# Moving 74 of the 266 weight-residual subtractions from VectorE to GpSimd in a two-layer encoder kernel

## The reference

```python
def trunk(x, p, ...):
    for i in range(DEPTH):                       # DEPTH = 2
        if i % N_MIXERS == 0:                    # layer 0: gated short convolution, two big matmuls
            y, nh = short_conv_mixer(x, conv_states[j], a_w_in[j], a_conv_w[j], a_w_out[j])
        else:                                    # layer 1: trailing means over 2/4/8/16 frames, small matmuls
            y, nh = pool_mixer(x, pool_states[j], pos0, b_w_grp[j], b_scale[j])
        h = layer_norm(ALPHA * x + y, ln1_g[i], ln1_b[i])
        r = jax.nn.relu(h @ mlp_w1[i])           # 1024 -> 4096
        f = (r * r) @ mlp_w2[i]                  # 4096 -> 1024
        e = (p[i] @ ple_w[i]) * jax.nn.sigmoid(h @ ple_gate_w[i])
        x = layer_norm(ALPHA * h + f + e, ln2_g[i], ln2_b[i])
```

## Time and profile before

| | |
|---|---|
| time, median of 3 runs | 2246.59 us (2242.61 to 2251.49) |
| the profiled execution | 2246.59 us, span 2244.8 us |
| PE busy | 2144.8 us (96%), 13166 matmuls |
| DVE busy | 1237.4 us (55%) |
| ACT busy | 779.6 us (35%) |
| POOL busy | 72.9 us (3%) |
| mean granted PE clock | 0.982 of 2.4 GHz |

### The profile page before, as it was taken

How to read it: one execution, slowest core, us unless ns; L and a number is a source line. 1 busy time by engine, 2 the same in 40 slices (tenths; PEclk the granted TensorE clock), 3 DMA queues, 4 the chain that set the end, 5 groups by cost and what they waited for, 6 DMA issues and landing times.

```text
span 2244.8 us, 32406 instructions
## 1 busy us (share of the span) xinstructions
PE 2144.8 (96%) x13166; PEld 2124.4 (95%) x13166; DVE 1237.4 (55%) x1795; ACT 779.6 (35%) x1203; POOL 72.9 (3%) x61
## 2 busy tenths in 40 slices
PE   8999999899999999999998988789999999999987
PEld 8999999899999999999998988789999999999986
DVE  4233368753444434445667879894354444444587
ACT  3222134542232222234443555353233332223354
POOL 0000000000000000000002003200000000000000
PEclk9999999999999999999999999899999999999998
DMA  4011142321111111113312233233122211112232
GB/s 164 29 56 53 41 132 69 104 92 57 57 57 38 50 43 48 46 47 118 127 48 63 83 119 93 66 102 100 57 76 66 66 57 57 38 57 75 76 112 97
DMA packets 47403, 164.69 MB, mean 73 GB/s; under 512 B 7488, under 2 KB 7616, under 8 KB 47296
## 3 DMA queue, kind: packets, MB, share of 16 engines
q1 hardware_dynamic: 45216, 163.04, 22.9%
q10 hardware_dynamic: 2080, 0.12, 0.1%
HBM read 158.68 MB, written 4.46 MB: 73 GB/s over the span
## 4 chain that ended last, share of the span: by engine, by line
PE 81%; DVE 13%; ACT 4%; issue 2%; DMA 0%; ACTq 0%; DVEq 0%
PE ps L645 27%; PE ps L647 27%; PE ps L646 27%; DVE w_split L571 3%; ACT w_split L750 1%; DVE acc L990 1%; DVE acc L1007 1%; DVE acc L1070 1%; DVE ln_squares L959 1%; DVE std L999 1%; ACT acc L809 1%; DVE win L1023 1%; DVE r_lo L1066 1%; DVE ln_squares L960 0%; DVE h_hi L1029 0%
## 5 line engine op out<-in xcount | busy, mean ns | idle before, releaser
L645 PE MATMUL ps<-h_hi,w_split 128*128 128x352 f32 x2160 | 701.8, 325 | 24.6 <-DVE w_split L571 10.5
L647 PE MATMUL ps<-h_hi,w_split 128*128 128x352 f32 x2160 | 695.2, 322 | 0.0
L646 PE MATMUL ps<-h_lo,w_split 128*128 128x352 f32 x2160 | 695.1, 322 | 0.0
L645 PE MATMUL ps<-r_hi,w_split 128*128 128x352 f32 x1632 | 541.4, 332 | 40.5 <-DVE acc L1070 38.2
L646 PE MATMUL ps<-r_lo,w_split 128*128 128x352 f32 x1632 | 530.5, 325 | 0.0
L647 PE MATMUL ps<-r_hi,w_split 128*128 128x352 f32 x1632 | 530.1, 325 | 0.0
L1070 DVE TENSOR_TENSOR acc<-acc,ps 128x352 f32<-128x352 f32 x768 | 375.2, 518 | 144.0 <-PE ps L647 143.2
L645 PEld LDWEIGHTS ps<-h_hi,w_split 128*128 128x128 f32 x2160 | 407.5, 189 | 28.2 <-issue 12.7
L646 PEld LDWEIGHTS ps<-h_lo,w_split 128*128 128x128 f32 x2160 | 408.5, 189 | 0.4
L647 PEld LDWEIGHTS ps<-h_hi,w_split 128*128 128x128 f32 x2160 | 407.8, 189 | 0.0
L571 DVE TENSOR_TENSOR w_split<-w_raw,w_split 128x1024 fp32r<-128x1024 f32 x266 | 323.9, 1236 | 118.3 <-ACT w_split L750 118.1
(11 more groups left out here) (80 smaller groups left out, 1131.8 us busy)
## 6 DMA issues: line engine op xcount, KB each, us to landing
w_raw<-w_stream SPq DMA_DIRECT2D x290, 512.0 KB, 3.7
x_raw<-x_t SPq DMA_DIRECT2D x6, 704.0 KB, 8.5
y_t<-acc SPq DMA_DIRECT2D x4, 704.0 KB, 4.5
w_raw<-p_t SPq DMA_DIRECT2D x6, 352.0 KB, 2.9
y_t<-acc SPq DMA_DIRECT2D x4, 352.0 KB, 2.2
pool_new<-acc ACTq DMA_DIRECT2D x2, 60.0 KB, 5.8
vec<-vectors SPq DMA_DIRECT2D x1, 78.0 KB, 7.2
pool_history<-pool_hist SPq DMA_DIRECT2D x1, 60.0 KB, 6.9
```

The source lines that it names most:

```text
L645: pe.matmul(out, wh, mov_h, start=first, stop=False)
L646: pe.matmul(out, wh, mov_l, start=False, stop=False)
L647: return pe.matmul(out, wl, mov_h, start=False, stop=last)
```

## The change

Two of the three tables that say which engine subtracts are changed. The call sites that use `dve` stay as they are.

```diff
-    dve, both, first_two = (lambda j: "dve"), (lambda j: "dve"), (lambda j: "dve")
+    dve, both, first_two = (lambda j: "dve"), (lambda j: ("dve", "pool")[j % 2]), (lambda j: ("pool", "dve")[j // 2])
```

## The result

The changed kernel took 2260.36 us (median of 11 runs, 2254.62 to 2278.09) and the kernel before 2248.05 (11 runs, 2242.61 to 2255.11): a ratio of 1.006, 95% interval 1.004 to 1.0081, or +13.5 us (+9 to +18). The forecast was 2246 us, from a sum of -0.8; the measured time lies at the upper end of the whole range told (2231 to 2262) and outside that of the likeliest case (2237 to 2256).

A forecast was written before the change was run, and what follows sets the result against it. DVE was taken to set the end in the norm and pooling stages, PE everywhere else. Terms -3.9 - 3.1 + 2.6 + 1.5 + 1.3 + 0.8 = -0.8 us took 2246.6 to 2245.8, told as 2246 us, range 2231 to 2262.

The forecast's parts named there:

- the likeliest case: Whole kernel: 2246 us, own range 2237 to 2256, chance 0.56.
- last norms: From 2130 to 2200 us: a unit ahead of a sum costs 0.9, one behind wins 1.2; 0 (-1.2 to +1).
- gates of layer 0: Gate stage paced by DVE: subtraction and its wait leave DVE's loop, PE restarts earlier; -3.9 us (-5.5 to -2).
- quiet stretches: 475 to 1100 and 1515 to 2120 us, where PE never waits: 36 moved subtractions change nothing, 0 us.
- first norm, with its clock: First norm between the layers: POOL's turns delay the sum PE waits for, +2.6 us, and a lower clock follows, +1.5.
- pooling of group 0: A subtraction ahead of the four window additions at 1186.59 lengthens the DVE chain beside them; +1.3 us (-1.2 to +2).
- gates of layer 1: Second gate stage: the same gain with other norms beside it, partly hidden behind ACT; -3.1 us (-5 to -1).
- long stretch, groups 1 and 2: 1344 to 1486 us, pooling and norms: 12 units leave DVE, -14.8, POOL's lock returns 15.6; +0.8 us (-14.8 to +5.6).
- the duration: POOL's time for one moved subtraction, scaled by elements from a window addition of 732 elements at 1.40 us: 1.96 us.
- The price of the lock: DVE time lost to each POOL subtraction: 0 to 1.7 us, taken as 1.3 in the stretch of groups 1 and 2.
- so its time is PE's time: 1344 to 1486 us: DVE is busy 130.6 of 142 us, so 12 subtractions leaving it count fully for PE, -14.8.
- The second rival: Between 1105 and 1515 us POOL starts early and holds up DVE's sums and products, 1.7 us each; 2263 us, chance 0.18.

The follow-up runs named there:

- e13: The changed kernel with ALU.add instead of ALU.subtract in POOL's 74 instructions; 2261.6 us, ratio to before 1.0029 to 1.0066.
- e14: The changed kernel with the raw buffer as both inputs of POOL's subtraction; 2242.07 us (one run).
- e15: The changed kernel with POOL's subtraction written over two rows of 512 elements; 2259.17 us (one run).
- e9: The changed kernel with each of the 74 POOL subtractions written as two instructions of 512 columns; 2256.66 us, ratio to before 0.9997 to 1.0036.
- e7: The changed kernel with each of the 74 POOL subtractions written as four instructions of 256 columns; 2244.33 us, ratio to before 0.9959 to 1.0002.
- e12: The kernel before with only the window additions each written as two instructions; 2246.13 us, ratio to before 0.996 to 0.9997.
- e10: The kernel before with 8 gate subtractions, in quarters, and 10 at the last norms, whole, moved to POOL; 2235.95 us, ratio to before 0.9923 to 0.997.
- e11: As e10, with each window addition also written as two instructions; 2231.34 us, ratio to before 0.9879 to 0.9936.
- e8: The changed kernel with POOL subtracting only 840 of 1024 columns, the rest of the residual left out; 2248.11 us, ratio to before 0.9988 to 1.0011.
- e1: The kernel before with only the 8 subtractions of the two gate stages moved to POOL; 2242.03 us, ratio to before 0.9939 to 0.9985.
- e4: The changed kernel with the 22 subtractions in the visits between the layers given back to DVE; 2244.91 us, ratio to before 0.9958 to 1.0004.
- e5: As e4, plus 22 extra POOL subtractions of the same size, each started once DVE has done that unit itself; 2264.3 us (one run).
- e3: The changed kernel, but each POOL subtraction also waits until DVE reaches its old place in the order; 2256.78 us, ratio to before 1.0016 to 1.0064.
- e6: As e5, but the 22 extra POOL instructions are memsets of the raw buffer, which write SBUF and read nothing; 2240.34 us (one run).

## Why the subtraction takes 2.39 us

**e13_add**, **e14_same** and **e15_two_rows** each make POOL's instruction like a window addition in one respect. In e13 and e14 the `lo` part of these weights is not the residual. Shown are the instruction's arguments alone, the last line in short:

```diff
-ws[:, slot, 1, :], raw[:, u.q, :], f32(ws[:, slot, 0, :]), ALU.subtract
+ws[:, slot, 1, :], raw[:, u.q, :], f32(ws[:, slot, 0, :]), ALU.add        # e13
+ws[:, slot, 1, :], raw[:, u.q, :], raw[:, u.q, :], ALU.subtract           # e14
+all three .rearrange("p (a t) -> p a t", a=2), ALU.subtract               # e15
```

> The changed kernel with ALU.add instead of ALU.subtract in GpSimd's 74 instructions (so the residual part of these weights is wrong). If the operation is what makes the subtraction dearer per element than the window additions (128x256, 512, 840, 1024 took 0.73, 1.27, 1.96, 2.38 us, 2.15 ns an element; window additions of 366 and 732 took 0.80 and 1.40, 1.64 ns an element), it takes 1.9 us and the kernel 2246 to 2250 us. If not, 2.39 us and 2257 to 2263 us.

> The changed kernel with the raw buffer as both inputs of GpSimd's subtraction (so the residual part of these weights is zero). If two inputs from tensors far apart cost more than two from one, it takes 1.9 us; if not, 2.39.

> The changed kernel with GpSimd's subtraction written over two rows of 512 elements, as the window additions go over two rows of 366. If the shape matters, 1.9 us; I expect 2.39, as the pieces of 256 and 512 had the same cost per element.

POOL's group from 500 to 1000 of e14, then of e15, e9 and e7:

```profile
L1162 POOL TENSOR_TENSOR w_split<-w_raw 128x1024 fp32r<-128x1024 f32 x2 | 3.8, 1896 | 156.9 <-ACT w_split L750 156.9
```

```profile
L1163 POOL TENSOR_TENSOR w_split<-w_raw,w_split 128x1024 fp32r<-128x1024 f32 x2 | 4.8, 2394 | 155.9 <-ACT w_split L750 155.9
```

```profile
L578 POOL TENSOR_TENSOR w_split<-w_raw,w_split 128x512 fp32r<-128x512 f32 x4 | 5.1, 1292 | 155.3 <-ACT w_split L757 155.3
```

```profile
L578 POOL TENSOR_TENSOR w_split<-w_raw,w_split 128x256 fp32r<-128x256 f32 x8 | 5.6, 738 | 154.8 <-ACT w_split L757 154.8
```

Neither the operation (e13: 2.39 us too) nor the shape matters; the inputs do. With one tensor as both inputs the instruction takes 1.90 us. The window additions read one tensor twice, shifted; a subtraction reads two tensors far apart. Subtractions grow by 2.15 ns an element ((2.39 - 0.74) / 768) above a base of 0.19 us, window additions by (1.40 - 0.80) / 366 = 1.64 (0.80 us for one of 366 elements in e12). Whether it is the distance of the two addresses or the tensor was not tried.

## A version that beats both

**e10_gates_last** keeps on POOL the 8 units of the gates, in quarters, and the 10 at the last norms, whole. **e11_windows_too** also writes each window addition as two instructions, and **e12_windows** does only that, in the kernel before.

```diff
-                    ins = pool.tensor_tensor(dst[:, :, have:end], src[:, :, have:end], src[:, :, have - lag:end - lag], ALU.add)
+                    for b in range(2):
+                        ins = pool.tensor_tensor(dst[:, b, have:end], src[:, b, have:end], src[:, b, have - lag:end - lag], ALU.add)
```

> Only the 8 subtractions of the gate stages (in quarters) and the 10 at the last norms (whole) are on GpSimd, the other 56 are back on VectorE. Sum from the earlier traces: gates in quarters -5.8 and -5.2 + 0.9, last norms -3.0, nothing between the layers: -13 us, some 2236 us. Rival: the quarters win in the gates only together with the units between the layers, then -6 - 3, 2239 us.

> As the kernel with gates and last norms on GpSimd, and each of the 30 window additions, which stood on GpSimd before as well, written as two instructions, one for each of its two blocks (366 elements instead of 732). Theory F: VectorE's waits behind them (18 instructions longer by 22.3 us between 1340 and 1500 before) come down by a third or more; PE gets back 3 to 8 us there, 2228 to 2233 us. Rival H (the window chain itself is late, and two instructions take longer than one): PE waits for the group matmuls, 0 to +5 us.

> The kernel before with nothing but the window additions in two pieces. Theory F: the same 3 to 8 us as beside the moved subtractions, 2240 to 2245 us. Rival H: 2248 or slower.

e10 came out as summed up, 2235.95 for 2236; by the ratio it wins 11.9 us (7 to 17) for the 13 expected. The windows in halves win 5.2 us between beside e10 and 6.4 by themselves (4.7, 1 to 9, by the ratio of e12), and DVE's waits behind them fall from 32.9 to 28.1 us although there are 49 of them for 27. e11 is the fastest kernel seen, 2231.34 us, 0.9% under the kernel before.

## Why the forecast was wrong, by its own steps

Each term by the starts of PE's matmuls, in us. e13 and e15 are two more executions with a POOL instruction of 2.39 us; e8 and e14 have one of 1.99 and 1.90, the forecast's duration (1.96) put to the test.

| term | forecast | changed (e13, e15) | e8, e14 | e7 |
|---|---|---|---|---|
| gates of layer 0 | -3.9 | -3.5 (-3.5, -3.5) | -4.5, -4.8 | -6.6 |
| quiet stretches | 0 | 0.0 (1.2, 0.0) | 5.1, 0.0 | 1.2 |
| first norm, with its clock | +2.6 + 1.5 | +5.9 (6.3, 6.1) | +2.4, +2.4 | +0.6 |
| pooling of group 0 | +1.3 | +3.1 (5.0, 5.0) | +1.3, +2.4 | -0.9 |
| gates of layer 1 | -3.1 | -3.9 (-3.9, -3.9) | -4.0, -4.3 | -5.8 |
| long stretch, groups 1 and 2 | +0.8 | +10.5 (13.0, 13.0) | +7.1, +5.9 | +7.0 |
| last norms | 0 | -3.0 (-3.0, -1.4) | -1.8, -3.4 | -1.4 |
| sum without the quiet stretches | -0.8 | +9.2 (14.0, 15.4) | +0.7, -1.9 | -7.1 |

(The 5.1 of e8 in a quiet stretch comes without a wait of PE: matmuls there take 0.160 us each for 0.159, at a granted clock of 1.00. e10 has the same, with no subtraction on POOL in that stretch, and e9 7.2 in the other one; most kernels here have none, and what it is stays open. In e1 and e4, without a subtraction on POOL in the visits between the layers, pooling is +2.4 and +1.0 and the long stretch +1.4 and +1.3: so much of these rows is not POOL's. The last norms are -1.3 in e12 too, where no unit moved, and the changed kernel, e7, e8 and e14 lose 1.2 us again behind them: at most some 2 us are the change's. The sum of the changed kernel is low for its +13.5 us by the ratio, as that execution was its fastest; e13 and e15 are nearer.)

**The step that failed is the duration**: "by elements a subtraction of 1024 would take 1.96 us". It took 2.39, since the row it was scaled from reads one tensor and not two. With about the forecast's own duration the sum is +0.7 or -1.9 for the forecast's -0.8, and the time 2248.1 us (e8) for its 2246. The 0.4 to 0.5 us are in every term that rests on POOL's length: first norm and pooling together +5.4 forecast, +3.7 and +4.7 at the short duration, +9.0 to +11.3 at the long one. The right size was on record: the prediction names 2.5 us and "some 10 us dearer" beside its 1.96, and takes the scaled row. Of its signs of being wrong, "over 2.5 us" is met by the page's mean (2.55, with POOL's own waits in it) but not by the 2.39.

**The relief was priced too high**, and that is hidden in the sum. The price of the lock was about right at the forecast's duration: in the long stretch DVE's waits grew against e4 by 16.4 us in e8 and 15.4 in e14, for 12 units 1.4 and 1.3 each, where I had 1.3; with 2.39 us they grew by 20.7, 1.7 each. Yet the stretch is +7.1 and +5.9 in e8 and e14 for a forecast of +0.8. What fails is the step before: "so its time is PE's time", by which the 1.24 us that leave DVE with each unit were all credited to PE. In e5, which takes nothing off DVE, 20.9 us of waits were 21.5 us of PE. If waits count whole in the others too, the 27.2 us taken off DVE gave PE some 12 to 20 (an estimate: growth of the waits less growth of *between*, both against e4, in e3, e8, e13, e14, e15 and the changed kernel, as 34.8 - 17.2 = 17.6 in the last). No run takes units off DVE without a cost on POOL, so this is argued and not shown. The last norms and the other terms made it good in the sum, so that -0.8 and its +0.7 agree in part by luck.

**The second rival** (POOL jumps DVE's queue, 2263 us) came nearest, and its condition, a mean price above 1.3 us, was met: against e4 the waits grew by 34.8 us for 22 units, 1.6 each. But its mechanism is the smaller part: e3 takes the jumping away and keeps +10.5 of +15.6 between. The length of the instruction did most of the rest: at the short duration, with the jumping left in, the kernel's time is that of the kernel before (e8, ratio 0.9999).

**The place**: right at the first norm in kind, wrong in detail (both subtractions got ahead of the sum, and I had the second behind it). e3 puts a price on it, +10.5 against +15.6 between, from one execution each. The waits of the earlier trace rows were the right model, and the L1070 row too: its mean did not move.

**Right**: both gate stages (-3.9 and -3.1 forecast, -3.5 and -3.9 read), the quiet stretches, and which DVE instructions are held up, but for the cast L1029, which the prediction does not name. The Trainium skill, "GPSIMD Engine Reference", introduction, has GpSimd at half of VectorE's speed in elementwise work; the trace agrees, 2.39 to 1.24 us. Section 3.1 of that page of the Trainium skill names reading two inputs through one port as what sets GpSimd's pace in a `tensor_tensor`; e14 fits it only in part, for it has two inputs as well and is faster. The Trainium skill, "SBUF — State Buffer", section on who interferes with whom, exempts a GpSimd instruction that only writes; e6 agrees, 37.4 us of waits for e4's 37.5.

## What to carry to other kernels

Before work moves to an engine that shares a port with the busy one, price it by a row with the same operands, not only the same operation and size; then ask of each place whether the other engine is waited for there, because the same move won 8.5 us in the gates and lost 19 in the visits. Where two engines take turns on a lock, cut the long instruction of the one that nobody waits for: four pieces of 0.74 us cost DVE half as much per meeting as one of 2.39. An instruction that starts when its data come, and no longer in its old place in a queue, jumps ahead of what stood before it.

## What the hardware showed that I had not expected

- POOL's two-input instruction depends on where the inputs lie: 2.39 us from two tensors, 1.90 from one (128x1024, float32).
- A waiting POOL instruction got its turn between two DVE instructions that follow each other at once (1107.02 to 1107.29), and did so twice in one chain of three sums; DVE did not keep the ports for its chain.
- A one-input cast on DVE waits for POOL (L1029, 726 to 1320 ns in the mean; all 9 beside a POOL addition or subtraction were longer), a reciprocal of one input (2346 to 2344, 3 beside one) does not.
- A POOL memset of 128x1024 takes 0.95 us and held up nothing on DVE that was beside it; no cast was.
